# Causal mask of latent attention: a product on TensorE in place of an addition on VectorE

## What is computed

```python
def block(i):
    start = i * Q_BLOCK                       # Q_BLOCK = 128
    qs = lax.dynamic_slice_in_dim(q_lat, start, Q_BLOCK, axis=1)
    qr = lax.dynamic_slice_in_dim(q_rope, start, Q_BLOCK, axis=1)
    s = (jnp.einsum('bqhr,bkr->bhqk', qs, ckv)
         + jnp.einsum('bqhe,bke->bhqk', qr, krope)).astype(jnp.float32) * MLA_SCALE
    qpos = start + jnp.arange(Q_BLOCK)
    s = jnp.where(key_pos[None, :] <= qpos[:, None], s, -jnp.inf)
    p = jax.nn.softmax(s, axis=-1).astype(ckv.dtype)
    return jnp.einsum('bhqk,bkr->bqhr', p, ckv)
```

## Time and profile before

| | us |
|---|---|
| median of 3 runs | 1305.96 (1303.84, 1305.96, 1311.23) |
| profiled execution, its own time | 1308.22 |
| profiled execution, span from first to last instruction | 1306.5 |
| TensorE busy in the span | 1239.2 (95%) |
| VectorE busy in the span | 830.2 (64%) |
| ScalarE busy in the span | 561.7 (43%) |

### The profile page before, as it was taken

How to read it: one execution, slowest core, us unless ns; L and a number is a source line. 1 busy time by engine, 2 the same in 40 slices (tenths; PEclk the granted TensorE clock), 3 DMA queues, 4 the chain that set the end, 5 groups by cost and what they waited for, 6 DMA issues and landing times. The chain is left out here.

```text
span 1306.5 us, 24471 instructions
## 1 busy us (share of the span) xinstructions
PE 1239.2 (95%) x9634; PEld 1173.3 (90%) x9634; DVE 830.2 (64%) x1324; ACT 561.7 (43%) x925; POOL 171.1 (13%) x217
## 2 busy tenths in 40 slices
PE   6999999999898998999999999999999999999996
PEld 6988777899767887999999999999999999999996
DVE  4122222344797778766897777777657665668977
ACT  4212323233654446644754445444464233322435
POOL 3514333110000000123000000000000000000552
PEclk9999999999898998999999999999999999999998
DMA  8749888433311011531346877868587555554103
GB/s 291 234 137 299 271 287 279 154 105 98 108 57 44 3 50 34 184 94 46 106 141 219 286 268 284 283 243 299 194 293 262 200 185 195 194 188 140 61 20 111
DMA packets 116536, 226.91 MB, mean 174 GB/s; under 512 B 13203, under 2 KB 60581, under 8 KB 114118
## 3 DMA queue, kind: packets, MB, share of 16 engines
q1 hardware_dynamic: 110278, 208.57, 46.8%
q0 software_dynamic: 6144, 16.79, 4.1%
HBM read 165.54 MB, written 58.73 MB: 172 GB/s over the span
## 5 line engine op out<-in xcount | busy, mean ns | idle before, releaser
L2828 PE MATMUL psum<-step_hid_hi,step_w_hi 128*128 128x258 f32 x784 | 159.1, 284 | 3.5 <-DVE y_sums L2867 2.7
L2828 PE MATMUL psum<-step_hid_hi,step_w_lo 128*128 128x258 f32 x784 | 158.5, 284 | 0.0
L2828 PE MATMUL psum<-step_hid_lo,step_w_hi 128*128 128x258 f32 x784 | 157.9, 283 | 0.0
L355 PE MATMUL psum<-xTh,win_hi 128*128 128x344 f32 (+1 forms) x432 | 147.9, 342 | 10.0 <-DVE xTl L408 10.0
L355 PE MATMUL psum<-xTh,win_lo 128*128 128x344 f32 (+1 forms) x432 | 139.5, 323 | 0.0
L355 PE MATMUL psum<-xTl,win_hi 128*128 128x344 f32 (+1 forms) x432 | 139.4, 323 | 0.0
L2828 PEld LDWEIGHTS psum<-step_hid_hi,step_w_hi 128*128 128x128 f32 x784 | 122.8, 191 | 3.9 <-DVE step_w_lo L2803 2.9
L2828 PEld LDWEIGHTS psum<-step_hid_hi,step_w_lo 128*128 128x128 f32 x784 | 121.9, 190 | 0.0
L2828 PEld LDWEIGHTS psum<-step_hid_lo,step_w_hi 128*128 128x128 f32 x784 | 121.6, 190 | 0.0
L2445 PE MATMUL psum<-x_t_hi,w_variant_hi 128*128 128x258 f32 x512 | 103.9, 284 | 5.3 <-DVE hid_variants L2562 2.9
L2790 ACT ACTIVATE step_hid_hi<-step_hid_raw 128x2064 fp32r<-128x2064 f32 x21 | 40.6, 1934 | 151.7 <-PE psum L2828 136.8
(11 more groups left out here) (421 smaller groups left out, 3002.2 us busy)
## 6 DMA issues: line engine op xcount, KB each, us to landing
step_hid_raw<-hid_rows SPq DMA_DIRECT2D x21, 1032.0 KB, 7.5
k_pages<-in_pages SPq DMA_DIRECT2D x128, 160.0 KB, 3.1
v_pages<-in_pages POOLq DMA_DIRECT2D x128, 128.0 KB, 4.4
w_raw<-in_w SPq DMA_DIRECT2D x16, 1024.0 KB, 5.2
hid_rows<-hid_variants SPq DMA_DIRECT2D x28, 516.0 KB, 3.6
step_w_raw<-w_sums SPq DMA_DIRECT2D x12, 1024.0 KB, 5.2
hid_rows<-hid_variants SPq DMA_DIRECT2D x14, 774.0 KB, 5.1
step_w_raw<-in_w SPq DMA_DIRECT2D x9, 1024.0 KB, 5.1
```

Of the source, the lines that this page charges most:

```text
L355: mm = pe.matmul(psum[0:M, 3 * (m % 2) + b, 0:BLK], w[:, m % 2, k, 0:M], x[:, k, b * BLK:(b + 1) * BLK], start=(k == 0 and i == 0), stop=( ...
L2828: mm = pe.matmul(slot(d)[:, s, :], wt[r][:, w], ht[r][:, TH * f + s * BW:TH * f + (s + 1) * BW], start=(f == 0 and i == 0), stop=(f == G - ...
```

## The change

In each row TensorE issues one more product between the two rotated parts of the scores' last piece: the unit matrix as the loaded operand and the mask as the moving one, 128 columns, summed into the same PSUM place on the diagonal. VectorE's addition (L1770) goes, and the maximum is the first instruction of a row on VectorE. Both operands must be fp32r, so ScalarE makes two copies (128×128 each) once, ahead of the loop, and TensorE waits for them before row 0.

```diff
@@ placement in SBUF
+        identr, causalr = (sb(at + P * i, n, [P, P], F32R) for i, n in enumerate(("ident_r", "causal_r"))); at += 2 * P
...
+        masks_in, MASKS_IN = cqsq_done, 5
@@ act_mla_in
             head_hi(act, 0)
+            act.activation(identr[:], ident, ACT.Copy).then_inc(masks_in, 1)
+            act.activation(causalr[:], const("causal"), ACT.Copy).then_inc(masks_in, 1)
             gb.wait(act, ("gT", 7))
             hi_of(act, "uv")
@@ pe_mla, scores(v)
                     if h == 0:
+                        pe.wait_ge(masks_in, MASKS_IN)
                         split(pe, "kr")
...
                     pe.matmul(s[:, p, :], qrs[:, HEAD[h], qc], krh[:, kc], start=False, stop=False)
+                    if p == nb - 1:
+                        d = 0 if i == 0 else w - P
+                        pe.matmul(s[:, p, d:d + P], identr[:], causalr[:], start=False, stop=False)
                     mm = pe.matmul(s[:, p, :], qrs[:, HEAD[h], qc], krl[:, kc], start=False, stop=True)
@@ dve_mla
                     dve.wait_ge(sc_full, v + 1)
-                    diag = s[:, 0, 0:P] if i == 0 else s[:, nb - 1, w - P:w]
-                    dlink(dve, dve.tensor_tensor(diag, diag, const("causal"), ALU.add))
                     dlink(dve, dve.tensor_reduce(stat[:, v % 4, 0:1], sc_used(v), AX.XY, ALU.max))
```

## The result

The changed kernel takes 1298.78 us (median of 20 runs, 1294.02 to 1303.2) against 1307.21 us of the kernel before (20 runs): ratio 0.9938, 95% interval 0.9927 to 0.995. The forecast was 1304.5 us, 0.1% less than before, with 1300.0 to 1309.5 as its range. (The forecast was taken off the median of three runs, 1305.96; that of twenty is 1.25 us higher.)

The account below looks back on a forecast made before the run. TensorE and VectorE were taken to bound the loop by turns; 32 masks off VectorE (10.4 us ceiling) against 32 products (3.7 us) summed stretch by stretch to -1.5 us, 1304.5 us off the median 1305.96, range 1300.0 to 1309.5.

Parts of the forecast that it names:

- What bounds the loop: Loop over 32 rows: neither engine bounds all; TensorE leads at projections or value products, VectorE at each head's long last rows.
- Product 0.115 us: Each new mask product on TensorE costs 0.115 us, bounds 0.05 and 0.23; the 32 cost 3.7 us of its time.
- Mask 0.325 us on VectorE: Each addition removed from VectorE frees 0.325 us; 32 make 10.4 us, the ceiling of the gain.
- Copies hidden: Ahead of the loop, ScalarE's two copies take some 0.55 us inside its 2.96 us idle time and add nothing.
- The sum, -1.5 us at a clock held as it was: Shifts from masks and products, carried stretch by stretch through the rows, leave TensorE about 1.5 us earlier at the loop's end.
- Rival 2: Masks lead everywhere in the loop: 20 masks and some 10 products on the path, -5.4 us, 1300.6 us; chance 0.12.
- The stalls: TensorE's stalls in the loop: those of row 6's and row 22's transposes would be about 1.5 us.
- the one at 456.13: TensorE's stall at 456.13 us in the loop, behind rows 9 to 13; it would be gone.
- Idle time in the loop: TensorE's idle time in the loop would fall from 13.4 to about 8 us, mostly filled by its new products.
- rival 3: Clock in the loop: one 1.2 GHz stretch fewer or more, up to 3 us, 1301.5 or 1307.5; chance 0.15, two thirds faster.
- so the 1.5 us are handed on: Behind the loop TensorE is busy without a gap, so the loop's 1.5 us gain reaches the kernel's end.
- the low-clock share of the loop differs clearly from 0.92: Sign that the prediction is wrong: the loop's granted clock, mean 0.92 before, clearly differs in the new profile.

Follow-up runs that it names:

- e2: The changed kernel without the mask's products, so neither addition nor product and the causal mask left out: 1297.88 us, ratio 0.9933 to the kernel before.
- e4: The changed kernel with the mask's product issued twice in every row: 1301.73 us, ratio 0.9961 to the kernel before.
- e1: The kernel before, VectorE's additions kept, with 40 unread filler products of 256 columns in TensorE's stalls: 1301.3 us, ratio 0.9957.
- e6: The kernel before with 40 filler products of 256 columns ahead of rows 4, 5, 12 and 20, where TensorE doesn't stall: 1310.13 us, ratio 1.0029.
- e16: The kernel before with 32 unread products of 16 columns ahead of row 0, in TensorE's wait for `v_lo`: 1304.29 us, ratio 0.9991.
- e17: The kernel before with 32 unread products of 16 columns behind the `y_sums` wait, in that stage's last step: 1318.41 us (two runs), ratio 1.009.
- e18: The kernel before with 6 unread products of 16 columns ahead of row 0 instead of 32: 1305.96 us, ratio 0.9995.

## Why the prediction was wrong

- *What bounds the loop*: held. TensorE and VectorE lead by turns. Removing 10.4 us of VectorE's work alone gave 4.7 us of the loop (e2).
- *Product 0.115 us*: 0.11 on the timeline, 0.08 to 0.10 of the loop's time by e4 and e2. Right.
- *Mask 0.325 us on VectorE*: its busy time in the loop fell by 8.9 us, where 9.3 were busy in the additions. Right.
- *Copies hidden*: right.
- *The sum, -1.5 us at a clock held as it was*: 1.4 to 2 us by the profiles. The mechanism was right and its size right or a little small. Rival 2 (-5.4 by masks alone) did not happen: e2, with no mask on either engine, gave 4.7 us where rival 2's 20 masks are 6.5. That the measured 1298.78 us is nearer to its 1300.6 than to the forecast is chance; the gain came from elsewhere.
- *The stalls*: 1.69 at row 6 and at row 22 where about 1.5 was forecast; the one at 456.13 didn't go but fell to 0.22. Idle time in the loop 9.1 us instead of 8.
- **The first step that failed: the clock.** The sum gave no term to a change of the stretches at 1.2 GHz, and rival 3 priced one "stretch of 6 us less" at up to 3 us with a chance of 0.1. In fact the profiled executions went from 20.5 to 3.4 us, the means of four from 14.5 to 4.3: three stretches of about 3.4 us fewer, worth about 4 us. The facts for it stood in the trace of before, though not in the rows of the forecast: three of the four stretches begin at 425.5, 459.7 and 493.8, at the end of the stalls of 2.34 and 1.87 us and in the pair of 2.12 and 1.01 us, all of which the forecast shortened itself. e1 against e6 shows the mechanism.
- **The second: "so the 1.5 us are handed on".** They were, but I had looked at 74 us behind the loop and took the other 700 for unchanged because the code is. 3.5 us were gained there by a shifted code load (e16, e17, e18).
- Its own sign "the low-clock share of the loop differs clearly from 0.92" is what came true.

What stays open: why one stall is followed by 1.2 GHz and its like isn't. Behind the stalls of 1.87 and 2.12 us the clock fell, and behind 1.69 (428.01) it didn't. But it fell behind 1.72 and 0.51 us at the start of the changed kernel's loop (402.2), and in two of the other three traces of before it didn't fall behind the stalls that are like those of 2.34 and 1.87. Idle time alone doesn't decide it either: in e17 it fell within a group of products of 16 columns without a wait. So the gain of one execution can't be forecast stall by stall; what the runs show is the mean. Also open is the rest of the wait at 442 us.

## What to carry to other kernels

Where the page shows a granted clock under 1.00 in a stage with short stalls of the engine that bounds it, price each stall twice: its own length, and the time at 1.2 GHz behind it; profile a kernel several times before trusting either. A few products that nobody reads, placed in the stalls, tell how much of a stage is clock, and a control with the same products elsewhere tells it from a shift of the code. Take off what the control's products cost on the path, and compare the mean clocks of the runs and not only one profile each. When code that wasn't touched gets faster, compare the DMA view of one late transfer with its instruction packets in both traces.

## What was not expected of the hardware

- 40 products that nobody reads made the kernel 0.43% faster (e1), the same number elsewhere 0.29% slower (e6); both hold 3.5 us gained by the code load.
- The clock fell to 1.2 GHz 2.8 us into 32 products of 16 columns, with TensorE never idle (e17, 1238.5).
- A single 0.02 MB instruction packet inside a 1 MB transfer goes with a landing 1.1 us later: 8.4 to 8.7 us in 7 traces, 7.3 to 7.7 in 13. One comes for every 256 of TensorE's records.
- A 128×128 load with a product of 16 columns repeats every 0.11 us (e16) to 0.13 us (e17), no faster than one with 128 columns.
